# Last network of a fused transformer pair: inner product of strip pairs by seven products of quarters

## What is computed

```python
m = _rmsnorm(h, norm_mlp_g[l])
hid = jnp.square(jax.nn.relu(jnp.einsum('bsd,df->bsf', m, w_mlp_in[l])))
h = h + jnp.einsum('bsf,fd->bsd', hid, w_mlp_out[l])
return _rmsnorm(h, norm_final_g)
```

## Time and profile before

| | |
|---|---|
| median of the runs | 3551.57 us |
| span of the profiled execution | 3549.7 us; its own time is not listed, the median lies 1.9 us above the span |
| busy: PE / weight loads / DVE / ACT / POOL | 98% / 79% / 33% / 33% / 36% |
| chain that ended last | PE 87%, of it 57% at L1937, which is `product` |
| mean granted clock of TensorE | 0.994 |
| DMA | 295 MB, 83 GB/s |

### The profile page before, as it was taken

One profiled execution on the slowest core, in us unless ns is written; L12 is line 12 of the kernel. 1 busy time (PEld: TensorE's weight loads), 2 busy tenths in 40 slices (PEclk: granted clock), 3 DMA queues, 4 the chain that ended last, 5 costly groups with the idle time before them and its releaser, 6 DMA issues.

```text
span 3549.7 us, 44638 instructions
## 1 busy us (share of the span) xinstructions
PE 3479.2 (98%) x18870; PEld 2812.2 (79%) x18870; DVE 1180.2 (33%) x1503; ACT 1180.5 (33%) x1652; POOL 1292.3 (36%) x696
## 2 busy tenths in 40 slices
PE   7999999999999999999999999999999999999998
PEld 5888887777778878888888878888887888888886
DVE  6333325535335774111111343033283221111113
ACT  5333324343324472211212355233323340212133
POOL 2311114434322753332323654211123662424265
PEclk9999999999999999999999999999999999999999
DMA  4211213221335422111112333213333331111133
GB/s 120 75 55 55 66 49 111 67 90 54 115 101 204 137 78 83 48 48 51 50 48 68 95 111 119 63 60 99 118 123 108 107 97 51 48 48 48 54 95 113
DMA packets 417029, 295.48 MB, mean 83 GB/s; under 512 B 12832, under 2 KB 385440, under 8 KB 416832
## 3 DMA queue, kind: packets, MB, share of 16 engines
q1 hardware_dynamic: 386592, 246.50, 23.0%
q10 hardware_dynamic: 30240, 46.14, 3.8%
HBM read 245.25 MB, written 47.35 MB: 82 GB/s over the span
## 4 chain that ended last, share of the span: by engine, by line
PE 87%; DVE 3%; ACT 3%; POOL 3%; issue 2%; DMA 0%; SPq 0%; POOLq 0%; ACTq 0%; DVEq 0%
PE psum L1937 57%; PE psum L266 14%; PE psum L1577 5%; PE psum L1093 2%; PE psum L572 2%; POOL w_lo L1888 1%; PE psum L1624 1%; ACT w_hi L1871 1%; PE psum L1174 1%; POOL m_lo L2051 0%; PE psum L1614 0%; PE psum L2666 0%; PE psum L1086 0%; DVE conv L2392 0%; DVE acc L2205 0%
## 5 line engine op out<-in xcount | busy, mean ns | idle before, releaser
L1888 POOL TENSOR_TENSOR w_lo<-w_raw,w_hi 128x1024 fp32r<-128x1024 f32 (+1 forms) x359 | 858.1, 2390 | 1868.4 <-ACT w_hi L1871 1854.8
L1871 ACT ACTIVATE w_hi<-w_raw 128x1024 fp32r<-128x1024 f32 (+1 forms) x363 | 378.4, 1043 | 1113.6 <-PE psum L1937 1087.5
L1937 PE MATMUL psum<-x_hi,w_hi 128*128 128x512 f32 x1840 | 642.8, 392 | 1.4 <-DVE w_lo L1897 1.0
L1937 PE MATMUL psum<-x_hi,w_lo 128*128 128x512 f32 x1840 | 638.1, 389 | 0.0
L1937 PE MATMUL psum<-x_lo,w_hi 128*128 128x512 f32 x1840 | 638.0, 389 | 0.0
L1937 PEld LDWEIGHTS psum<-x_hi,w_hi 128*128 128x128 f32 x1840 | 345.1, 188 | 76.5 <-issue 5.7
L1937 PEld LDWEIGHTS psum<-x_lo,w_hi 128*128 128x128 f32 x1840 | 345.4, 188 | 73.6 <-issue 2.2
L1937 PEld LDWEIGHTS psum<-x_hi,w_lo 128*128 128x128 f32 x1840 | 345.4, 188 | 71.9
L266 PE MATMUL psum<-x_hi,w_hi 128*128 128x512 f32 x832 | 360.7, 434 | 7.2 <-ACT gate L310 3.7
L266 PE MATMUL psum<-x_hi,w_lo 128*128 128x512 f32 x832 | 327.9, 394 | 0.0
L266 PE MATMUL psum<-x_lo,w_hi 128*128 128x512 f32 x832 | 326.6, 393 | 0.0
(11 more groups left out here) (573 smaller groups left out, 5364.3 us busy)
## 6 DMA issues: line engine op xcount, KB each, us to landing
w_raw<-in_w_in SPq DMA_DIRECT2D x105, 512.0 KB, 4.4
w_raw<-in_w_ffn_up SPq DMA_DIRECT2D x56, 512.0 KB, 3.7
merge_raw<-gates ACTq DMA_DIRECT2D x48, 512.0 KB, 3.9
w_raw<-in_w_mlp_in SPq DMA_DIRECT2D x48, 512.0 KB, 4.0
w_raw<-in_w_mlp_out SPq DMA_DIRECT2D x40, 512.0 KB, 4.0
gates<-gate SPq DMA_DIRECT2D x32, 512.0 KB, 3.0
w_raw<-in_w_ple_gate SPq DMA_DIRECT2D x16, 512.0 KB, 4.1
w_raw<-in_w_ffn_down SPq DMA_DIRECT2D x16, 512.0 KB, 3.9
```

Source lines behind the costliest of these rows:

```text
L1871: act.activation(self.view(self.c.wh, i), self.view(self.c.wr, i), ACT.Copy).then_inc(self.sig["w_hi"], 1)
L1888: pool.tensor_tensor(self.view(self.c.wl, i), self.view(self.c.wr, i), self.view(self.c.wh, i).bitcast(F32), ALU.subtract).then_inc(self.s ...
L1937: last = pe.matmul(self.bank(t, h)[0:m, :], w[:, k, col:col + m], x(k)[:, 512 * h:512 * h + 512], start=(k == 0 and n == 0), stop=(k == nk ...
```

## The change

The first chunk shrinks to four strips of w_in (two pairs, numbers 0 and 1), taken by halves, with the products of pair 0 by w_out behind each half (`tensor_first`, `tensor_early`). The other fourteen pairs of strips are multiplied as 2x2 blocks: two strips by two halves of the inner width on the side of the weights, two halves of the inner width by two halves of the tokens on the side of x. The seven products of the Winograd form of Strassen's scheme take the place of eight (`Mlp.tensor_in`), each of 4 inner tiles x 3 = 12 matmuls.

This needs sums of quarters. For x they are made once, in the head: POOL puts together again the first half's x from its high and low part (`Halves.rebuild`), DVE forms four differences for each of four inner tiles (`Halves.sums`), ACT rounds them (`hi`, `last_hi`) and DVE makes the low parts (`lo`, `last_lo`). The second half's scaled x now goes to SBUF rather than PSUM. For the weights POOL forms four sums in every pair (`Feed.sums_of`, `Feed.lo`). `Feed` replaces `Stream` there: blocks of 128x512 in six raw and five split places. On the side of the results DVE adds the products up with two running sums and squares in place (`vector_in`).

Outputs are no longer 1024 deep: after pair p comes the product of pair p-1 by its 256 rows of w_out, added to `acc` by DVE (16 tiles of 128x512 for each pair). Pairs 14 and 15 are done together at the end, a half at a time (`tensor_last`), with the final norm beside and behind them (`LastNorm`). Two loads of the residual now share a semaphore, and DVE waits for both.

The diff, cut to its core. Its last hunks are, in this order, the programs of ACT, of DVE and of POOL in `second_group`.

```diff
     def residual_in(self, sp, k):
         self.ready(sp, k)
-        sp.dma_start(self.c.a[:, k, :], self.residual[k * P:k * P + P, :]).then_inc(self.sig[f"residual{k}"], 16)
+        sp.dma_start(self.c.a[:, k, :], self.residual[k * P:k * P + P, :]).then_inc(self.sig[f"residual{k // 2}"], 16)
...
             return
         if h == 0 and self.residual is not None:
-            dve.wait_ge(self.sig[f"residual{m}"], 16)
+            dve.wait_ge(self.sig[f"residual{m // 2}"], 32)
         elif h == 0:
...
+class Feed:
+
+
+
+    PLACES, SLOTS = 5, 6
+    SEVEN = ("a11", "s2", "s3", "s1", "a12", "s4", "a22")
+
...
+    def pair(self, q, block_of):
+
+        r11, r21, r22, r12 = (self.load(block_of(n, k), 4) for n, k in ((0, 0), (1, 0), (1, 1), (0, 1)))
+        self.added[q] = [self.step() for _ in range(3)]
+        us = []
+        for name in self.SEVEN:
+            r = {"a11": r11, "a12": r12, "a22": r22, "s3": r21, "s4": r12}.get(name)
+            u = self.block(name, q, r, 4)
+            us.append(u)
+            at = self.split_at(u)
...
+    def hi(self, act, u):
+        if u >= len(self.blocks):
+            return
+        name, q, r, nk, summed, at, _ = self.blocks[u]
+        if u < self.PLACES:
+            self.free.place(act, u)
+        else:
+            act.wait_ge(self.sig["f_mm"], self.blocks[u - self.PLACES][6])
+        if summed:
+            act.wait_ge(self.sig["f_pool"], summed)
+        else:
+            self.arrived(act, r)
+        act.activation(self.places[u % self.PLACES][0], self.raw(u), ACT.Copy).then_inc(self.sig["f_hi"], 1)
...
+    def sums_of(self, pool, u):
+
+        q, r11 = self.blocks[u][1:3]
+        r21, r22 = r11 + 1, r11 + 2
+        slot = lambda r: self.slots[r % self.SLOTS]
+        if u < self.PLACES:
+            self.free.sums(pool)
+        for r in (r11, r21, r22):
+            self.arrived(pool, r)
+        s1, s2 = self.sums
+        n = self.added[q][0]
+        self.add(pool, slot(r21), slot(r22), s1, ALU.add, n - 1)
+        self.add(pool, s1, slot(r11), s2, ALU.subtract, n)
+        self.add(pool, slot(r11), slot(r21), slot(r21), ALU.subtract, n + 1)
...
+    def lo(self, pool, u):
+        if u >= len(self.blocks):
+            return
+        name, q, r, nk, summed, at, _ = self.blocks[u]
+        if name == "a11":
+            self.sums_of(pool, u)
+        hi, lo = self.places[u % self.PLACES]
+        pool.wait_ge(self.sig["f_hi"], u + 1)
+        pool.tensor_tensor(lo, self.raw(u), hi.bitcast(F32), ALU.subtract).then_inc(self.sig["f_pool"], 1)
+        if name == "a12":
+            self.add(pool, self.raw(u), self.sums[1], self.raw(u), ALU.subtract, at)
...
+    def tensor_early(self, pe, h):
+        for hh, m, t, i in self.early[KT * h:KT * h + KT]:
+            self.st.product(pe, t, i, lambda k: self.hh(k), lambda k: self.hl(k), P * (m % 4), halves=(h,),
+                            before=None if m else (lambda k: pe.wait_ge(self.sig["h_lo"], 4 * h + k + 1)))
...
+    def tensor_in(self, pe, p):
+        sig, feed = self.sig, self.feed
+        for n, ((u, e), x) in enumerate(zip(self.pairs[p], self.ORDER)):
+            feed.ready(pe, u)
+            if p == 2 and n in (0, 2):
+                self.st.freed(pe, n // 2)
+            if n == 3:
+                pe.wait_ge(sig["s1"], p - 1)
+            else:
+                self.summed(pe, self.FREES[n], p - 1 if n < 3 else p)
+            if p == 2 and n in (1, 6):
+                pe.wait_ge(sig["quarter_lo"], 12 if n == 1 else 16)
+            x_hi, x_lo = self.x[x]
+            wh, wl = feed.cubes(u)
+            for k in range(KT // 2):
+                for i, (w, v) in enumerate(((wh, x_hi), (wh, x_lo), (wl, x_hi))):
+                    last = pe.matmul(self.c.ps[:, n % 3, :], w[:, k, :], v(k), start=(k == 0 and i == 0),
+                                     stop=(k == KT // 2 - 1 and i == 2))
+            last.then_inc(sig["f_mm"], 1)
...
+    def tensor_last(self, pe, h, between):
+        for c, (u0, u1, tiles) in enumerate(self.outs["last", h]):
+            self.feed.ready(pe, u0)
+            if h == 0 and c == 0:
+                pe.wait_ge(self.sig["h_lo"], self.split(self.PAIRS - 2))
+            for m, _, e, n in tiles:
+                self.free(pe, n)
+                ins = self.products(pe, u0, self.PAIRS - 2, m, h, n, True, False)
+            ins.then_inc(self.sig["f_mm"], 1)
+            self.feed.ready(pe, u1)
+            if h == 0 and c == 0:
+                pe.wait_ge(self.sig["h_lo"], self.split(self.PAIRS - 1))
+            for m, _, e, n in tiles:
+                self.products(pe, u1, self.PAIRS - 1, m, h, n, False, True).then_inc(self.sig["f_mm"], 1)
...
+        def add(i, x, out):
+            self.done(dve, ends[i])
+            dve.tensor_tensor(out, banks[i], x, ALU.add).then_inc(sig["summed"], 1)
+
+        def square(name, h):
+            self.summed(dve, name, p)
+            self.squared(dve, h, h).then_inc(sig["summed"], 1)
+
+        dve.wait_ge(sig["s1"], n)
+        add(1, s1, u2)
+        self.summed(dve, "u2", p)
+        add(2, u2, u3)
+        self.summed(dve, "u3", p)
+        add(3, u3, h22)
+        add(3, u2, u2)
+        square("c22", h22)
+        add(4, s1, h11)
+        square("c11", h11)
+        add(5, u2, h12)
+        square("c12", h12)
+        add(6, u3, h21)
+        square("c21", h21)
...
+    def scalar_in(self, act, p):
+        for n, (u, e) in enumerate(self.pairs[p]):
+            if n == 0:
+                self.first_product(act, p)
+            if n >= 4:
+                self.scalar_quarter(act, p, n - 4)
+            self.feed.hi(act, u + Feed.PLACES)
...
+    def pool_in(self, pool, p):
+        for n, (u, e) in enumerate(self.pairs[p]):
+            self.feed.lo(pool, u + Feed.PLACES)
+            if n >= 4:
+                self.pool_quarter(pool, p, n - 4)
...
+    def rebuild(self, pool, i):
+
+        self.rms.done(pool, 0, 4 + i)
+        if i == 0:
+            self.st.done(pool, self.rms.tiles[1])
+        for k, dst in ((i, self.raws(i)[0]), (4 + i, self.kept[:, i, :])):
+            pool.tensor_tensor(dst, self.c.xh[:, k, half(0)].bitcast(F32), self.c.xl[:, k, half(0)].bitcast(F32), ALU.add
+                               ).then_inc(self.sig["x_again"], 1)
+
+    def sums(self, dve, i):
+
+        t1, t2, t3 = self.raws(i)
+        kept = self.kept[:, i, :]
+        self.rms.done(dve, 1, 4 + i)
+        dve.wait_ge(self.sig["x_again"], 2 * i + 2)
+        dve.tensor_tensor(t1, t3, t1, ALU.subtract).then_inc(self.sig["quarter"], 1)
+        dve.wait_ge(self.sig["quarter"], 4 * i + 1)
+        dve.tensor_tensor(t3, t2, t3, ALU.subtract).then_inc(self.sig["quarter"], 1)
+        dve.wait_ge(self.sig["quarter"], 4 * i + 2)
+        dve.tensor_tensor(t2, t2, t1, ALU.subtract).then_inc(self.sig["quarter"], 1)
+        dve.wait_ge(self.sig["quarter"], 4 * i + 3)
+        dve.tensor_tensor(kept, kept, t2, ALU.subtract).then_inc(self.sig["quarter"], 1)
+
+    def hi(self, act, i):
+        act.wait_ge(self.sig["quarter"], 4 * i + 4)
+        for name, raw in zip(("t1", "t2", "t3"), self.raws(i)):
+            act.activation(self.x[name][0](i), raw, ACT.Copy).then_inc(self.sig["quarter_hi"], 1)
+
+    def lo(self, dve, i):
+        for n, (name, raw) in enumerate(zip(("t1", "t2", "t3"), self.raws(i))):
+            dve.wait_ge(self.sig["quarter_hi"], 3 * i + n + 1)
+            dve.tensor_tensor(self.x[name][1](i), raw, self.x[name][0](i).bitcast(F32), ALU.subtract
+                              ).then_inc(self.sig["quarter_lo"], 1)
+
+    def last_hi(self, act):
+        self.st.done(act, self.last_first())
+        for i in range(4):
+            act.wait_ge(self.sig["quarter"], 4 * i + 4)
+            act.activation(self.x["t4"][0](i), self.kept[:, i, :], ACT.Copy).then_inc(self.sig["quarter_hi"], 1)
+
+    def last_lo(self, dve):
+        for i in range(4):
+            dve.wait_ge(self.sig["quarter_hi"], 12 + i + 1)
+            dve.tensor_tensor(self.x["t4"][1](i), self.kept[:, i, :], self.x["t4"][0](i).bitcast(F32), ALU.subtract
+                              ).then_inc(self.sig["quarter_lo"], 1)
...
+    def square(self, act, n, m, h):
+
+        i = self.squares
+        self.squares += 1
+        act.wait_ge(self.sig["added"], n + 1)
+        if i >= 2:
+            act.wait_ge(self.s("sum"), i)
+        act.activation(self.c.square[:, half(i % 2)], self.c.a[:, m, half(h)], ACT.Square).then_inc(self.s("sq"), 1)
...
+    def deviation_last(self, act):
+        r = self.rstd[:, :]
+        act.wait_ge(self.s("total"), 2)
+        act.wait_ge(self.s("warm"), 1)
+        act.activation(r, self.c.ps[:, 1, :], ACT.Ln, bias=self.eps).then_inc(self.s("log"), 1)
+        act.wait_ge(self.s("log"), 2)
+        act.activation(self.c.ps[:, 2, :], r, ACT.Exp, scale=-0.5).then_inc(self.s("rstd"), 1)
+        act.activation(r, r, ACT.Exp, scale=-0.5).then_inc(self.s("rstd_pool"), 1)
...
+            for q in range(4):
```

(102 more changed lines are left out.)

458 lines of the change are left out of this document (303 added, 155 removed).

## The result

| | before | changed |
|---|---|---|
| median of 20 runs each, same chip | 3553.91 us (3551.52 to 3556.55) | 3559.62 us (3554.95 to 3563.36) |
| ratio | | 1.0016, 95% interval 1.0009 to 1.0023 |
| span of the profiled execution | 3549.7 | 3557.8 (own time 3559.55) |

The change makes the kernel 5.7 us slower; the forecast was 7.7, and 3559.3 in all. That is 0.16%, by size within the 0.2% that the prediction took for no change, by its interval nonetheless not zero. In the traces the network's first matmul stands at 2834.2 before and at 2836.8 after. Stretches are therefore compared from that zero: to the last logarithm it was 703.3, and is 709.1.

The account below looks back on a forecast made before the run. TensorE, busy 98% of the span, was taken as the bound. Terms -38.1 - 2.5 + 33.9 (head) + 4.4 (pair 15) + 5.7 (end) + 4.3 (clock) = +7.7 on 3551.6 gave 3559.3 us, range 3542 to 3571.

Parts of the forecast that it names:

- Removed, -38.1 and -2.5: In the last network, 168 fewer matmuls save 38.1 us, and old waits that disappear save 2.5.
- Head, +33.9 and 1.1 of clock: Before pair 2, PE waits for quarter preparation add 33.9 us; a slower clock after waits adds about 1.1.
- The turns: DVE operations with two SBUF inputs and POOL operations reading SBUF exclude each other for whole instructions: 1816 ns against 751.
- The ring: Head, second half: a chain over ACT, POOL and DVE takes 11.35 us from ReLU to ReLU, against PE's 5.44.
- Middle, nothing: Fourteen pairs in the loop: each takes 40.8 us at PE's own pace, with no added cost.
- The cover: Middle: the other engines' and load queues stay in step with PE, so their work adds nothing.
- Pair 15, +4.4 and 2.2 of clock: At pair 15, PE waits 4.4 us for the fourth quarter's split by POOL; a slower clock adds 2.2.
- End, +5.7 and 1.0 of clock: After the last product, the logarithm starts 8.5 us later instead of 2.8: +5.7; a slower clock adds 1.0.
- 1 (turns that cost little): Rival: DVE and POOL seldom meet in the head, so turns cost far less; 3527 us at full effect; chance 0.22.
- 2 (the same time): Rival: the clock costs nothing and the head two or three us less; 3552 to 3558 us; chance 0.30.
- 3: Rival: in the middle, blocks arrive late and each pair waits 1 us; 14 more, 3573 us; chance 0.06.
- The bound without any turns: Same order with no DVE and POOL exclusion: smaller waits and a 24 to 25 us faster kernel than before.

Follow-up runs that it names:

- port: Changed kernel with one operand of 32 DVE operations in the head read from an idle PSUM bank, not SBUF (values not right): 3542.22 us.
- addr: Changed kernel with only the added weight place `w_more` moved up by 128 bytes: 3554.51 us.
- q15: Changed kernel with POOL's program around pair 15 reordered: sums cleared earlier, hidden quarters ahead of weight blocks not yet due: 3555.53 us.
- tail: Changed kernel with the first half's norm root in a PSUM bank and `warm` not waiting for the scalings: 3555.67 us.
- head: Changed kernel with ACT, DVE and POOL reordered before pair 2 and the differences' results in three idle PSUM banks: 3546.29 us.

## Why the prediction held, and where it didn't

**Removed, -38.1 and -2.5:** both held. From zero to the last logarithm the changed kernel has 662.8 us of pure work (66.1 to pair 2, 2616 matmuls and one column sum behind it, 2.8 at the end), and the kernel before took 703.3: 40.5.

**Head, +33.9 and 1.1 of clock:** without any wait, 288 matmuls and one column sum put pair 2 at 66.1; predicted 101.1, measured 97.5, so the term is 31.4 instead of 35.0. The turns, as a mechanism, are shown by port: 18.3 of the 31.4. The ring was put 0.6 us a round too long (its terms as listed add up to 11.3, not 11.35), because one low part starts beside ACT's conversion, ahead of POOL's strip. PE's waits on the way are 3.7, 3.0, 0.6, 5.0 and 3.1 where 4.4, 5.5, 3.0, 5.9 and 5.9 were put. All those at L1937 are 20.6, less than the loss; forty matmuls at the pace of the 1.2 GHz level, 0.43 apart in place of 0.227, make 8 of the rest. One wait behind the ring, 4.4 for the slot (L3767), was put at 8.2.

**Middle, nothing:** this step failed, by little. "One pair is 84 + 96 matmuls, 40.8 us of PE" assumed that every weight place reads alike; it was 41.09, 3.8 over the stretch, and addr takes it away. The cover that the step did name (POOL, DVE, ACT in step) held: no wait in 553 us, although the squares took 0.99 us each and not the 0.7 that was named as a sign.

**Pair 15, +4.4 and 2.2 of clock:** 3.7 of wait (the sign asked for over 4), and about 1.6 for the half pace behind it. q15 gets 3.6 of it back.

**End, +5.7 and 1.0 of clock:** the logarithm 7.96 behind the last slot against 9.5 with its clock. Shown by tail, as a pair of edits: 4.4 back.

**The sum:** from zero to the last logarithm +7.7 predicted, +5.8 measured: head -3.6, middle and pair 15 +3.2, end -1.5. Errors of opposite sign partly cancel, so the forecast is nearer than its terms. That the predicted 3559.3 lies within 0.3 us of the measured median is luck: the forecast started from 3551.6, the median of three runs, where twenty give 3553.9, and its difference is 2.0 too large.

**The rivals:** 1 (turns that cost little) falls. A kernel in which it were true would lie where port does, at 3542, since port takes away the turns of 32 of the 40 operations; the changed kernel lies 17 us above. 2 (the same time) is where the difference lies by size, within 7 us, and the head did come out some 3 us cheaper; but the clock did cost, as q15 shows. 3 had the right place, the middle, but the wrong cause: nothing arrives late. The bound without any turns was added up wrongly: its terms give 26.3 us faster, not 24 to 25, which moves the 3527 of rival 1 to 3525 and leaves the forecast as it is.

## What to carry to other kernels

Saving matmuls pays only as far as the work that prepares the saving is hidden. Here 41 us were saved (matmuls and old waits) and 46 given back, all but 4 of it ahead of and behind the loop that saves them; 27 could be won back without touching the idea. Before DVE work is put beside busy POOL, see where both of its inputs lie: one in PSUM makes the same operation 0.68 us long instead of 1.5 to 2.7. Shorten the ring, that is the chain of operations over several engines that each tile must go round, and not the wait in front of it. And read the pace of matmuls for every place that holds weights: here a new place cost 0.29 us a pair until it lay as the old ones do.

## What was unexpected of the hardware

A weight place 128 bytes off the position of the other tiles, counted from a multiple of 1024, made its matmuls come 0.2328 us apart instead of 0.2267, without a wait in any view; the weight loads themselves last the same 0.19 us. The Trainium skill ("SBUF — State Buffer", section "SBUF: two separate sides") says that within the engines' side of SBUF only the port pair shared by VectorE and GpSimd contends, and that PE never waits on anyone. Read as a rule for the pace of matmuls it would let no place cost anything, and the table above says otherwise. Whether it is another engine that PE waits on there, or something within PE's own reading, no run here shows.

The clock: behind a stop of 3.73 us some eight matmuls came at the pace of the 1.2 GHz level; behind one of 1.64 us, in q15, they came 0.23 apart at a granted 1.00. So the shorter wait saved 1.5 us more than its difference. The length of the stop alone doesn't decide it, though: in head, 1.81 us ahead of pair 2 was followed by seven matmuls 0.43 apart (granted 0.50 from 2917 to 2919), while the 1.50 us before that, for a slot, was not.
